# Two-stack transformer forward pass: each 2 MB chunk of weights loaded by two 1 MB transfers

## The reference, cut to what matters

```python
mod = silu_c @ w_ada[l] + b_ada[l]                       # in both stacks: six vectors of 1024
...
logits = jnp.einsum('bnd,de->ben', h, w_router)
gate, idx = lax.top_k(jax.nn.softmax(logits, axis=1), cap)   # cap = 32 tokens of 256
xs = h[bi, idx]
a = jnp.einsum('becd,edf->becf', xs, w_g)                # each expert: 1024 x 1024
u = jnp.einsum('becd,edf->becf', xs, w_u)                # 1024 x 1024
y = jnp.einsum('becf,efd->becd', jax.nn.silu(a) * u, w_d)    # 1024 x 1024
```

## Time and profile before

| | us |
|---|---|
| median of 3 runs | 2911.82 (2910.58 to 2915.54) |
| the profiled execution, its own time | 2912.62 |
| its span, first to last instruction | 2910.4 |
| PE busy | 2645.1 (91%) |
| DVE busy | 974.1 (33%) |
| ACT busy | 563.5 (19%) |
| loads of chunks | 336 of 2048 KB, 711.25 MB moved in all |

### The profile page before, as it was taken

How to read it: one execution, slowest core, us unless ns; L and a number is a source line. 1 busy time by engine, 2 the same in 40 slices (tenths; PEclk the granted TensorE clock), 3 DMA queues, 4 the chain that set the end, 5 groups by cost and what they waited for, 6 DMA issues and landing times.

```text
span 2910.4 us, 28396 instructions
## 1 busy us (share of the span) xinstructions
PE 2645.1 (91%) x11372; PEld 1642.7 (56%) x11372; DVE 974.1 (33%) x2065; ACT 563.5 (19%) x1225; POOL 2.9 (0%) x8
## 2 busy tenths in 40 slices
PE   5999999999999999999997997988899997888787
PEld 4688888768887744544444342432377884233232
DVE  6612550541573244454633110110254333011010
ACT  2311120321212154310002011111354001000000
POOL 0000000000000000000000000000000000000000
PEclk9999999999999999999997999999999998999999
DMA  9614664623654310133432799999612746999998
GB/s 368 272 58 173 231 243 165 262 83 154 244 234 180 124 42 29 58 144 145 173 159 101 331 428 428 429 429 428 297 59 87 289 175 254 428 429 429 429 427 358
DMA packets 51517, 711.25 MB, mean 244 GB/s; under 512 B 5523, under 2 KB 7843, under 8 KB 8405
## 3 DMA queue, kind: packets, MB, share of 16 engines
q1 hardware_dynamic: 50902, 708.00, 59.3%
q0 software_dynamic: 512, 1.79, 0.2%
HBM read 708.72 MB, written 1.05 MB: 244 GB/s over the span
## 4 chain that ended last, share of the span: by engine, by line
PE 70%; DMA 22%; DVE 4%; ACT 3%; issue 2%; SPq 0%; ACTq 0%; DVEq 0%; PEldq 0%
PE bank L590 69%; DMA ring<-weights 22%; PE bank L589 1%; DVE ring L1372 1%; ACT work L1244 0%; ACT work L1252 0%; DVE X L1417 0%; DVE work L1398 0%; DVE work L1397 0%; DVE h L1408 0%; ACT work L1304 0%; DVE small L1595 0%; DMA cst<-const 0%; ACT work L1220 0%; ACT work L1219 0%
## 5 line engine op out<-in xcount | busy, mean ns | idle before, releaser
L590 PE MATMUL bank<-h,ring 128*128 128x256 f32 (+1 forms) x3840 | 1020.9, 426 | 31.3 <-ACT h L1113 29.0
L590 PEld LDWEIGHTS bank<-h,ring 128*128 128x128 f32 x3840 | 733.0, 192 | 305.1 <-issue 218.9
L590 PE MATMUL bank<-ring,work 128*64 128x512 f32 x3072 | 691.7, 598 | 136.7 <-DMA ring<-weights 130.1
L590 PEld LDWEIGHTS bank<-ring,work 128*64 128x64 f32 x3072 | 215.2, 137 | 586.9 <-issue 422.2
L590 PE MATMUL bank<-work,ring 128*128 128x256 f32 (+1 forms) x1728 | 456.4, 421 | 7.7 <-DVE X L1417 6.3
L590 PEld LDWEIGHTS bank<-work,ring 128*128 128x128 f32 x1728 | 328.8, 191 | 119.9 <-issue 83.1
L1723 DVE TENSOR_TENSOR work<-bank,work 128x512 f32<-128x512 f32 x32 | 22.1, 691 | 649.4 <-ACT work L1294 649.4
L1372 DVE SCALAR_TENSOR_TENSOR ring<-ring,crow 128x1024 f32<-128x1024 f32 x192 | 228.7, 1219 | 22.1 <-DMA ring<-weights 21.8
L590 PE MATMUL bank<-work 128*64 128x256 f32 (+4 forms) x1216 | 209.2, 383 | 26.6 <-ACT work L1244 10.3
L590 PEld LDWEIGHTS bank<-work 128*128 128x128 f32 (+2 forms) x1216 | 139.4, 180 | 88.2 <-issue 36.2
L1417 DVE SCALAR_TENSOR_TENSOR X<-bank,mod,X 128x256 f32<-128x256 f32 x152 | 67.9, 481 | 255.2 <-PE bank L590 254.6
(11 more groups left out here) (162 smaller groups left out, 1240.9 us busy)
## 6 DMA issues: line engine op xcount, KB each, us to landing
ring<-weights SPq DMA_DIRECT2D x336, 2048.0 KB, 19.7
X<-x_cols SPq DMA_DIRECT2D x1, 1024.0 KB, 18.0
X<-x_cols POOLq DMA_DIRECT2D x1, 1024.0 KB, 17.4
out<-X SPq DMA_DIRECT2D x2, 512.0 KB, 3.0
cst<-const SPq DMA_DIRECT2D x1, 914.5 KB, 4.8
cst<-const POOLq DMA_DIRECT2D x1, 512.0 KB, 23.5
pars<-par SPq DMA_DIRECT2D x1, 275.0 KB
work<-positions POOLq DMA_DIRECT2D x1, 128.0 KB, 7.7
```

What stands on the lines that cost most here:

```text
L590: nc.tensor.matmul(o, l, r, start=start, stop=stop)
```

## The change

`slot_full` becomes two semaphores for each slot, one for each half of the columns. Each chunk is loaded by two transfers of 128 partitions x 8 KB, one after the other in the same queue. PE's expert products wait for the half that they read; all other products of PE wait for both halves ahead of the first (`whole`). VectorE's sums wait for a half every two sums. When a slot comes free is as before.

```diff
-        self.slot_full = [ctx.enter_context(nc.semaphore(f"slot{s}_full")) for s in range(SLOTS)]
+        self.slot_full = [[ctx.enter_context(nc.semaphore(f"slot{s}_{half}_full")) for half in range(2)] for s in range(SLOTS)]
...
-    def loaded(self, c):
-        return self.slot_full[c % SLOTS], self.reg * (16 * (CHUNKS[self.name] // SLOTS)) + 16 * (c // SLOTS + 1)
+    def loaded(self, c, half):
+        return self.slot_full[c % SLOTS][half], self.reg * (16 * (CHUNKS[self.name] // SLOTS)) + 16 * (c // SLOTS + 1)
...
                     sp_.wait_ge(R.slot_used[s], i)
-                    sp_.dma_start(ring[:, s, :], weights[bass.ds(i * SLOTS + s, 1)].rearrange("a p c -> (a p) c"))\
-                       .then_inc(R.slot_full[s], 16)
+                    for half in range(2):
+                        cols = slice(half * CH // 2, (half + 1) * CH // 2)
+                        sp_.dma_start(ring[:, s, cols], weights[bass.ds(i * SLOTS + s, 1), :, cols].rearrange("a p c -> (a p) c"))\
+                            .then_inc(R.slot_full[s][half], 16)
...
+            def whole(c):
+
+                for half in range(2):
+                    pe.wait_ge(*R.loaded(c, half))
...
-                pe.wait_ge(*R.loaded(R.chunk("lat")))
+                whole(R.chunk("lat"))
...
                     for i in parts:
                         c = R.chunk("gu", 4 * e + i)
-                        pe.wait_ge(*R.loaded(c))
                         for kk in range(2):
+                            pe.wait_ge(*R.loaded(c, kk))
                             k = 2 * i + kk
...
                         c = R.chunk("dn", 2 * e + kh)
-                        pe.wait_ge(*R.loaded(c))
                         for j in range(4):
+                            if j % 2 == 0:
+                                pe.wait_ge(*R.loaded(c, j // 2))
...
                     c = R.chunk(name, t // 4)
-                    if n == 0 or jobs[n - 1][1] // 4 != t // 4:
-                        dve.wait_ge(*R.loaded(c))
+                    if n == 0 or jobs[n - 1][1] // 2 != t // 2:
+                        dve.wait_ge(*R.loaded(c, t % 4 // 2))
```

More of the change, by code:

```diff
@@ L548, in _ @@
             for s in range(SLOTS):
-                sp_.dma_start(ring[:, s, :], weights[s]).then_inc(R.slot_full[s], 16)
+                for half in range(2):
+                    cols = slice(half * CH // 2, (half + 1) * CH // 2)
+                    sp_.dma_start(ring[:, s, cols], weights[s, :, cols]).then_inc(R.slot_full[s][half], 16)
                 if s == 1:
@@ L652, in first_stack @@
                     c = R.chunk(job)
-                    pe.wait_ge(*R.loaded(c))
+                    whole(c)
                     for j in range(4):
@@ L667, in first_stack @@
                                      (R.bank("z", i)[:, T:384], [(ksb[:, i, P:T], qsb[:, i, P:T])])])
-                pe.wait_ge(*R.loaded(low))
+                whole(low)
                 pe.wait_ge(*lat_ready.take())
@@ L695, in first_stack @@
                 head_squares("ssk", 6, (10, 10))
-                pe.wait_ge(*R.loaded(vs))
+                whole(vs)
                 for i in range(2):
@@ L725, in both_gates @@
                     if t % 4 == 0:
-                        pe.wait_ge(*R.loaded(cm))
-                        pe.wait_ge(*R.loaded(cs))
+                        whole(cm)
+                        whole(cs)
                     bank = R.bank("gates", t)
@@ L763, in first_stack @@
                     if t == 0:
-                        pe.wait_ge(*R.loaded(wm))
-                        pe.wait_ge(*R.loaded(ws))
+                        whole(wm)
+                        whole(ws)
                         pe.wait_ge(*R.evac("mla_v", H1 - 1))
@@ L837, in dense @@
                 kv = R.chunk("kv")
-                pe.wait_ge(*R.loaded(kv))
+                whole(kv)
                 for job, i in dense_jobs(layer):
@@ L966, in branch @@
                 if t == 0:
-                    pe.wait_ge(*R.loaded(w))
+                    whole(w)
                     pe.wait_ge(*(R.evac("cb", 3) if b == "c" else R.evac("val" + b, nt // T * HB // 2 - 1)))
```

## The result

The changed kernel takes 2922.3 us (median of 8 runs, 2917.32 to 2924.96) against 2914.02 us (8 runs, 2910.58 to 2918.71) beside it: ratio 1.0025, 95% interval 1.0014 to 1.0035. A second measurement, with 12 runs and 29 of before, gave 1.0031 (1.0021 to 1.0041). 2922.3 lies in the range of 2906 to 2925; the single time, 2915.9, was 6.4 us short, of which 2.2 us are the kernel before, whose median is 2914.02 here and was 2911.82 when I predicted.

What follows compares the result with a forecast made beforehand. The DMA engines' packet rate bounds two expert stretches (178.5 chunks); elsewhere PE or a DVE and ACT chain does. Queue +10.1, ends -3.7, modulation -2.4 sum to +4.0 us: 2915.9 us, range 2906 to 2925.

Steps and rivals of the forecast that it cites:

- four places: Ends of the expert stretches in `y0` and `y1`, together -3.7 us, and the modulation in `b0` and `b1`, together -2.4 us.
- The time per packet: Load queue in both expert stretches: 9 more packets per chunk at 6.3 ns, 57 ns per chunk, +10.1 us over 178.5 chunks.
- no change that can be told: Whole kernel: likeliest case, 2907 to 2917.6 us, within about 0.2% of before, on the slow side; chance 0.52.
- the first rival: Load queue: per-packet or semaphore cost larger, from 67 ns per chunk on, slower by more than 0.2%; chance 0.33.
- The ends: Last loads in `y0` and `y1`: only half a chunk's products remain behind the last landing, -1.83 us each, -3.7 together.
- The modulation: Site "second" in `b0` and `b1`: VectorE's sums start by halves, saving PE's idleness, -1.26 and -1.09 us, together -2.4.
- The waits: PE's one or two more waits per chunk: cost 0 when already met, at most +3 us.
- SyncE: Issuing twice as many transfers: 0.9 us per chunk in place of 0.45, out of 4.9 us; cost 0.
- Bytes as the pace: Rival in the expert stretches: bytes, not packets, limit the queue, so no cost; -6.1 us, 2905.7 us; chance 0.10.
- A fixed cost of each transfer beyond its semaphore packet: Rival in the load queue: it stands still 2.6 us at each extra transfer, +464 us; chance 0.02.
- the descriptors' pace: Rival in the load queue: building rows takes about twice 9.2 ns and bounds, +0 to +10 us on top; chance 0.03.
- A larger cost per packet: Load queue: more than 67 ns per chunk, for example 95 ns giving 2922.6 us; chance 0.33.

Runs made afterwards that it cites:

- run 2: Against the kernel before: one transfer and one semaphore per chunk, but a gap in each slot's row makes rows of 8 KB; 2933.34 us, ratio 1.0061.
- run 4: Against the kernel before: four transfers of 512 KB per chunk, a semaphore each, all waits for the whole chunk; 2962.92 us, ratio 1.0167.
- Run 9: Against the kernel before: 16 chunks in halves, and in layer 1's expert stretch pairs of chunks in one 4 MB transfer, rows of 32 KB; 2906.28 us, ratio 0.9982.
- run 1: Changed kernel's loads in halves, but PE and VectorE wait for the whole chunk everywhere; 2927.63 us, ratio 1.0043 to the kernel before.
- run 3: Against the kernel before: only ten chunks in halves (`own` 8, 9 in `b0`, `b1`; last `gu`, last two `dn` in `y0`, `y1`); 2917.23 us, ratio 1.0004.

## Why the prediction came out as it did

**The mechanism** was right in its main parts: the queue slows by a time per row, four places give some back, the rest costs little. The sum at equal clock is +13.7 (178.5 x 77 ns), -3.5 (ends) and -2.7 (modulation), +7.5 us; the two ratios make it +7.3 and +9.0 us. That the sum meets the +7.4 of equal clock so closely is luck: the three levels of the clock gave 5.6 to 9.8, and the profiles have 1.7 us outside these terms.

**The time per packet** was the term that I sized too low: 57 ns per chunk predicted, 77 measured, +13.7 and not +10.1 us. I drew the line from 16 KB to 1 KB rows, 6.3 ns of it per packet. Runs 2 and 4 give 8.3 ns for one more row between 16 and 8 KB and 7.8 between 8 and 4 KB, and 11 ns for a second transfer with its semaphore, where I had put 6.3. Run 9 gives some 10 ns between 32 and 16 KB: (38 x 24 / 20 - 0.5 x 11) / 4. So the price of a row falls as rows get shorter, while the queue's share rises: 100.4% with pairs, 100.6% at 16 KB, 101.2% at 8, 102.7% at 4 and 109.1% at 1 KB. I take it that packets which overlap more hide part of their fixed time; no run tests that. The point at 1 KB was the wrong neighbour, and a window of 2 us a weak one: the same width 0.2 us later has 717 packets, which makes the price 6.8 ns. This alone moved the likeliest case from "no change that can be told" (0.52) to the first rival (0.33), whose threshold was 67 ns. The Trainium skill's 3 cycles per packet ("DMA: Bandwidth & Descriptors", "Why small descriptors are slow") are further off still: an estimate of 32 ns per chunk from its figure, against 77 measured.

**The ends** gave -1.8 us in layer 1: +6.9 from the queue and +5.1 measured. In layer 0, 88.4 x 77 ns = +6.8 less 1.7 is +5.1, and measured is +3.0; of the other 2.1, 1.5 us are the last two `dn` chunks, which took 8.61 us before and 7.09 after. The windows of before show the clock there:

```profile
2057.00:2061.00 4.00, 3.54 (x10) 1.14 (x12) 0.00 (x0) 0.41 (x1) 0.00 (x0) 0.57 1.03 436
```

Against run 1, with these places at half clock taken out, the change gains 1.9 us in layer 0's stretch and 2.0 in layer 1's. The amount was right, the name not: the chunk at 2050.70 us is the second `dn` chunk of the last but one expert, not the last `gu` chunk. That both have the same price was luck; run 3 was built on the name, and missed.

**The modulation** gave -1.4 and -1.3 us (from PE's products ahead of the site to those behind it) for -1.26 and -1.09 predicted: what PE had been waiting, not the 2.3 us by which L1448 could start sooner. It started 1.75 us sooner, as the last half comes at 91.09 us, later than the whole chunk before (90.56 us).

**The waits** cost nothing: 96 instructions for the first six chunks take 20.82 us after, as before.

```profile
1607.89 20.82 PE bank L594 x96
```

(This is the chain of waits of the changed kernel.) **SyncE** twice as often shows in the chain, for 1.3 us at a time, and costs nothing, since the share stays at 1.01:

```profile
2606.49 1.94 PE bank L594 x8
...
2609.38 26.87 DMA ring<-weights
2636.30 1.94 PE bank L594 x8
2638.67 1.33 SPq L563
```

**The rivals.** Bytes as the pace: out, by run 2, where the same bytes in twice the rows take 66 ns more. A fixed cost of each transfer beyond its semaphore packet, and the descriptors' pace: out, by run 4, where four transfers per chunk cost what their rows and semaphores cost. A larger cost per packet: this is what happened, mostly through the rows (8 of them took 66 ns, where I had put 50) and less through the second transfer with its semaphore (11 ns for 6.3).

Of the signs that I had named, the share, 8 instructions behind the last wait and the idle time in pieces half as long came as said; GB/s fell to 422 (423 +- 3 said), and a group of experts takes 119.3 us (1699.53 to 1818.84 in the chain), where I had said 118.9.

## What to carry to other kernels

Where a queue of loads is the bound, its price per row counts, and finer pieces help only where work starts behind the last landing. Here splitting those few chunks and leaving the rest whole took the loss away (ratio 0.9995), and longer rows in the stretch where the queue stays full made the kernel faster (0.9982). Price a row size that you haven't measured from a near one, not from the far end of a line: the line to 1 KB said 6.3 ns where halving the rows cost 8.3. And when a change is worth less than half a per cent, compare runs at the same granted clock, or stretches of the profile whose clock is the same; a change that gathers PE's idleness into longer pieces can cost it the clock, as both stretches of run 3 show.

## What the runs showed of the hardware

- A row costs 8.3 ns on its DMA engine beyond its bytes (16 to 8 KB), 7.8 from 8 to 4 KB, and the saving goes on to 32 KB (431 GB/s against 428). In a full queue rows of 4, 8, 16 and 32 KB (the last in 20 of 24 chunks) moved 410, 423, 428 and 431 GB/s.
- A second transfer with its semaphore costs 11 ns per chunk and engine in a full queue.
- TensorE's granted clock fell to half after single waits of 2.85 and 2.87 us and did not fall with waits of 1.2 us every 4.9 us. Elsewhere the length of the wait doesn't tell: behind 2.52 us of idleness the last two `dn` chunks of `y0` took 8.61 us in one kernel and 7.09 in another, and the same 48 instructions behind the same 1.04 us took 11.3 and 14.5 us, without a cause that I can name. Run times of one kernel go with their mean granted clock (2910.1 us at 0.981, 2917.5 at 0.978).
- With pairs PE waits up to 6.2 us in one piece in layer 1, and the mean clock of the stretch is 0.95, at no cost, as the queue is the bound there (share 1.00).
